# A query projection split in two passes, and an expert gather in groups of two rows

## The reference

```python
q = (hf @ w_q).reshape(T, 8, 2, 128)
s = einsum('thpd,hpnd->thpn', q, sub_keys)          # 128 scores per head and half
sc, idx = top_k(s, 16)                              # per half
cand = sc[..., 0, :, None] + sc[..., 1, None, :]    # 256 pair sums per head
top_sc, pos = top_k(cand, 16)                       # 16 experts per head, 128 per token
gate = softmax(top_sc)
act = gelu(einsum('thkd,td->thk', u_tab[eidx], h))
y = einsum('thk,thkd->td', gate * act, v_tab[eidx])
```

## Time and profile before

| what | value |
|---|---|
| median of 3 runs | 3951.03 us (3946.89 to 3958.45) |
| the profiled execution | 3955.62 us, span 3953.5 us |
| first gather issued / first dot | 2524.75 us / 2539.04 us |
| first dot into slot 8 or above | 2804.9 us (row 72) |
| last dot starts | 3913.04 us (row 511) |
| HBM traffic of the gathers | 536.90 MB |

### The profile page before, as it was taken

The page is one execution under the profiler, slowest core; times in us unless marked ns, Lnnn a source line. Parts: engine busy times, 40 slices in busy tenths (PEclk is TensorE's granted clock), DMA queues, the critical chain, the costliest instruction groups (busy, mean ns, idle before and its releaser), DMA issues. The chain is left out here.

```text
span 3953.5 us, 33526 instructions
## 1 busy us (share of the span) xinstructions
PE 3431.1 (87%) x12069; PEld 2132.3 (54%) x12069; DVE 2296.8 (58%) x4193; ACT 635.4 (16%) x1221; POOL 1878.5 (48%) x1174
## 2 busy tenths in 40 slices
PE   7987999998988999989999889887777777777877
PEld 5435947886655478866877667333333333333333
DVE  3834625445633154447935665456887777777564
ACT  2132222011115221111112331101010000000001
POOL 2212316886510168856877447123444444444442
PEclk9997999999989999999999889988889989999998
DMA  4430012222320123222432211567999999999995
GB/s 142 148 118 1 1 43 73 95 95 78 128 85 1 43 75 95 95 74 75 132 113 84 76 33 54 191 246 295 397 421 421 421 415 419 412 415 417 415 421 236
DMA packets 266249, 741.35 MB, mean 188 GB/s; under 512 B 12921, under 2 KB 192642, under 8 KB 200578
## 3 DMA queue, kind: packets, MB, share of 16 engines
q0 software_dynamic: 73728, 536.90, 33.3%
q1 hardware_dynamic: 188176, 196.15, 15.6%
q10 hardware_dynamic: 4210, 6.56, 0.4%
HBM read 731.17 MB, written 8.39 MB: 187 GB/s over the span
## 5 line engine op out<-in xcount | busy, mean ns | idle before, releaser
L796 POOL TENSOR_TENSOR split_arena<-weight_ring,ones 128x1024 fp32r<-128x1024 f32 x222 | 546.7, 2463 | 686.9 <-PE bank L891 322.6
L854 POOL DMA_INDIRECT arena<-in_peer_uv,rstd x364 | 412.2, 1132 | 643.0 <-PE bank L1354 554.4
L972 PE MATMUL bank<-split_arena 128*128 128x512 f32 x1776 | 698.0, 393 | 0.0
L2369 DVE CUSTOM_DVE_ANT_0 arena<-arena,branch 128x1024 f32<-128x1024 f32 x364 | 443.4, 1225 | 232.3 <-DMA arena<-in_peer_uv,rstd 229.2
L798 POOL TENSOR_TENSOR split_arena<-weight_ring,split_arena 128x1024 fp32r<-128x1024 f32 x222 | 546.2, 2460 | 17.4
L1354 PE MATMUL bank<-arena,level_mask 128*128 128x512 f32 x736 | 370.2, 661 | 109.4 <-DVE level_mask L2354 109.4
L970 PE MATMUL bank<-split_arena 128*128 128x512 f32 x1088 | 427.9, 393 | 17.8 <-DVE split_arena L1803 9.1
L1354 PE MATMUL bank<-arena,row_diagonals 128*128 128x512 f32 x720 | 346.5, 637 | 104.0 <-DVE row_diagonals L2354 104.0
L971 PE MATMUL bank<-split_arena 128*128 128x512 f32 x1088 | 425.1, 391 | 0.0
L972 PEld LDWEIGHTS bank<-split_arena 128*128 128x128 f32 x1776 | 335.5, 189 | 73.8
L891 PE MATMUL bank<-normed,weight_ring 128*128 128x512 f32 (+1 forms) x864 | 362.2, 578 | 5.0 <-DVE normed L1790 3.9
(11 more groups left out here) (346 smaller groups left out, 4937.0 us busy)
## 6 DMA issues: line engine op xcount, KB each, us to landing
weight_ring<-in_w_up SPq DMA_DIRECT2D x32, 1024.0 KB, 5.3
weight_ring<-in_w_down SPq DMA_DIRECT2D x32, 1024.0 KB, 5.1
weight_ring<-in_w_in SPq DMA_DIRECT2D x32, 1024.0 KB, 5.7
weight_ring<-in_ada_w SPq DMA_DIRECT2D x24, 1024.0 KB, 7.7
weight_ring<-in_w_in_a SPq DMA_DIRECT2D x13, 1024.0 KB, 5.3
weight_ring<-in_w_out SPq DMA_DIRECT2D x12, 1024.0 KB, 5.3
weight_ring<-in_w_in_b SPq DMA_DIRECT2D x10, 1024.0 KB, 5.2
weight_ring<-in_peer_wq SPq DMA_DIRECT2D x8, 1024.0 KB, 6.9
```

The costliest lines, as they stand in the source:

```text
L796: pool.tensor_tensor(hi, part, bc_mid(ones[:], DT), ALU.mult).then_inc(split_hi, 1)
L854: pool.indirect_dma_start(row_slots[slot_of[r]], None, a["peer_uv"], bass.IndirectOffsetOnAxis(ap=experts[n % 2][:, c:c + 1], axis=0)).the ...
L972: m = pe.matmul(psum[t.bank][:], hi[:, k, :], a_lo[:, k, :], start=False, stop=k == DT - 1)
L2369: dve.tensor_tensor_reduce(row, row, h_tok[:, r // NE, :], 1.0, 0.0, ALU.mult, ALU.add, dots[:, i % 4, j:j + 1]).then_inc(dot_ready, 1)
```

## The change

- `GROUP` is 2, so there are 256 groups, 64 in a block. `EARLY` is 136.
- The query projection is done twice over. First pass: all 8 units, with the 128 tokens of block 0 as the moving operand; four halves share a bank. Behind each pair of units come the scores of its heads. Second pass: the 8 units are loaded again (8 MB more), and the other 384 tokens are projected in 32 pieces of 4 matmuls, one piece after every second row group (groups 2 to 64).
- The normalised input is made in two parts: 128 columns first, then 384.
- Of the token-major copies of the input (`turn` of `H`) only block 0's is made ahead of the loop; the others come at groups 7 to 27.
- ScalarE evicts a piece, a turn or a score bank three groups after TensorE was to make it (`LAG`).
- Scores of blocks 1 to 3 come one pair of heads at a time, 16 groups apart; their searches run one piece in every second group. The searches of block 0 still to do run one piece per group at groups 0, 10 and 20.
- The sum of a block is taken 2 groups, turned 4 groups and added 8 groups after the block ends.

```diff
-GROUP = 4
+GROUP = 2
-EARLY = 64
+EARLY = 136
+LAG = 3
+PIECES = 8
...
+        query_at = {2 + 2 * y: y for y in range(2 * HP)}
+        turn_at = {7 + 4 * (2 * (n - 1) + i): (n, i) for n in range(1, TT) for i in range(2)}
+        score_at = {(BLK_GRP * (n - 1) + 16 * g + (20 if n == 1 else 28)): (n, g) for n in range(1, TT)
+                    for g in range(PH // SG)}
+        back_at = {BLK_GRP * (n + 1) + 4: n for n in range(TT - 1)}
+        take_at = {BLK_GRP * (n + 1) + 2: n for n in range(TT - 1)}
+        add_at = {BLK_GRP * (n + 1) + 8: n for n in range(TT - 1)}
...
-        for g, at in ((1, 0), (2, 5), (3, 9)):
-            search_at[0, g] = (at, 2)
-        for g in range(PH // SG):
-            search_at[1, g] = (14 + 4 * g, 2)
-            for n in range(2, TT):
-                search_at[n, g] = (BLK_GRP * (n - 1) + 8 * g + 1, 1)
+        search_at = {(0, 1): (0, 1), (0, 2): (10, 1), (0, 3): (20, 1)}
+        for n in range(1, TT):
+            for g in range(PH // SG):
+                search_at[n, g] = (BLK_GRP * (n - 1) + 16 * g + 32, 2)
...
-            for u in pq_units:
+            for u in first_units + rest_units:
                 load(u)
...
                 elif slot_of[r] >= 8:
-                    pool.wait_ge(half_done, 2 * (pq_units[-1].u + 1))
+                    pool.wait_ge(half_done, 2 * (rest_units[-1].u + 1))
...
+            def query_piece(y):
+                x, part = divmod(y, 2)
+                u, h, t = rest_units[x // 2], x % 2, rest_tiles[x]
+                if part == 0:
+                    pe.wait_ge(landed[u.slot], 16 * u.load)
+                    free(pe, t)
+                for k in range(part * DT // 2, (part + 1) * DT // 2):
+                    if x == 0:
+                        normed(k)
+                    m = pe.matmul(psum[t.bank][:, P:], block_of(u, k, h * P), H[:, k, P:], start=k == 0, stop=k == DT - 1)
+                if part:
+                    m.then_inc(half_done, 1)
+
+            for g, t in enumerate(first_tiles):
+                for x in range(2 * SG):
+                    u, h = first_units[SG * g + x // 2], x % 2
...
+                    for k in range(DT):
+                        if g == 0 and x == 0:
+                            normed(k)
+                        m = pe.matmul(blk(psum[t.bank], x), block_of(u, k, h * P), H[:, k, 0:P], start=k == 0, stop=k == DT - 1)
+                    m.then_inc(half_done, 1)
                 if g == 0:
-                    for n in range(TT):
-                        for i in range(2):
-                            turn(tok_turns[n][i], [blk(H[:, 4 * i + j, :], n) for j in range(4)])
+                    for i in range(2):
+                        turn(tok_turns[0][i], [blk(H[:, 4 * i + j, :], 0) for j in range(4)])
                 key_scores(0, g)
...
-            for i in range(2 * SG * 2):
+            for i in range(NGRP):
                 sum_rows(i)
-                query_tile(2 * SG * 2 + i)
+                if i in query_at:
+                    query_piece(query_at[i])
+                if i in turn_at:
...
+                if i in score_at:
+                    key_scores(*score_at[i])
...
             for i in range(NGRP):
                 act.wait_ge(dot_ready, GROUP * (i + 1))
                 act.activation(row_act[:, i % 4, :], dots[:, i % 4, :], ACT.Gelu).then_inc(gelu_ready, 1)
-                if i < 4 * SG:
-                    x = 4 * SG + i
-                    take(pq_tiles[x], pq_f[:, x, :])
+                if i - LAG in query_at and query_at[i - LAG] % 2:
+                    x = query_at[i - LAG] // 2
+                    t = rest_tiles[x]
+                    full(act, t)
+                    act.activation(pq_f[:, x, P:], psum[t.bank][:, P:], ACT.Copy).then_inc(bank_out[t.bank], 1)
...
-            modulate(1)
+            for cols in (slice(0, P), slice(P, SEQ)):
+                marks = []
+                for k in range(DT + 1):
...
-            for t in tok_turns[0] + tok_turns[1] + tok_turns[2] + tok_turns[3]:
-                have(dve, t)
             for _ in search(0, 0):
                 pass
```

More of the change, by code:

```diff
@@ L399, in build @@
             if g == 0:
[L400 to L405, removed]
-        for n in range(TT):
[L407 to L410, removed]
+                tok_turns[0] = [aux(2 + i) for i in range(2)]
@@ new lines, in build @@
+            peer_scores[0].append(aux(4 + g % 2))
+        rest_units = query_units()
+        rest_tiles = [half_tile(u, h, 6 + h) for u in rest_units for h in range(2)]
+        query_at = {2 + 2 * y: y for y in range(2 * HP)}
[3 more added lines that the diff above has]
+        back_at = {BLK_GRP * (n + 1) + 4: n for n in range(TT - 1)}
@@ L411, in build @@
+        peer_back.append([aux(2 * ((TT - 1) % 2) + i) for i in range(2)])
         norms.append(aux(4))
@@ L1333, in key_scores @@
                 free(pe, t)
-                for x in pq_tiles[4 * i:4 * i + 4]:
+                for x in rest_tiles[4 * i:4 * i + 4] if n else first_tiles[i:i + 1]:
                     have(pe, x)
@@ new lines, in _ @@
+            for g, t in enumerate(first_tiles):
+                for x in range(2 * SG):
+                    u, h = first_units[SG * g + x // 2], x % 2
+                    if h == 0:
+                        pe.wait_ge(landed[u.slot], 16 * u.load)
+                    if x == 0:
+                        free(pe, t)
+                    for k in range(DT):
[3 more added lines that the diff above has]
+                    m.then_inc(half_done, 1)
@@ new lines, in _ @@
+                if i in turn_at:
+                    n, x = turn_at[i]
+                    turn(tok_turns[n][x], [blk(H[:, 4 * x + j, :], n) for j in range(4)])
+                if i in score_at:
+                    key_scores(*score_at[i])
+                if i in back_at:
+                    n = back_at[i]
+                    for x in range(2):
+                        have(pe, row_sums[n][x])
+                        turn(peer_back[n][x], [y_sum[:, (4 * x + j) * P:(4 * x + j + 1) * P] for j in range(4)])
@@ L1393, in _ @@
+            for x in range(2):
+                have(pe, row_sums[TT - 1][x])
+                turn(peer_back[TT - 1][x], [y_sum[:, (4 * x + j) * P:(4 * x + j + 1) * P] for j in range(4)])
+            pre[0] += 1
             norm_sum(norms[5])
@@ L2367, in _ @@
                     row = row_slots[slot_of[r]][:, 0:D]
+                    if r % NE == 0:
+                        for t in tok_turns[r // NE]:
+                            have(dve, t)
                     dve.wait_ge(row_landed[slot_of[r]], 16 * fill[r])
```

119 lines of the change are left out of this document (55 added, 64 removed).

## The result

The changed kernel takes 3886.6 us (median of 4 runs, 3882.8 to 3889.9) against 3950.9 us for the kernel before on the same chip: a ratio of 0.9835, 95% interval 0.9816 to 0.9853. That is 1.65% faster, where 2.1% (3869 us) was forecast. The profiled execution took 3889.9 us with a span of 3888.2 us; before the span was 3953.5 us, so 65.3 us have gone where the prediction had 82.9.

A forecast was written before the change was run, and what follows sets the result against it. DMA engines bound it, at 2.524 us per gathered row: 2539.2 + 503 x 2.524 + 15 + 10 = 3833.8 us, + 36.8 = 3870.6 us span, + 2.1 = 3872.7 us profiled, so median 3869 us; range 3828 to 3940 us.

The forecast's parts named there:

- step 4: Rows 8 to 135 in eight slots: DMA-bound at 2.65 us a row, 15 us for second-pass bytes, 10 us for bursts.
- Step 1: Start of the gathers: block 0's input made first brings the search 23 us earlier, the first gather to 2501.6 us.
- Step 2: The first dot waits for unit 7, its load taken as 15.9 us: 2525 us, only 14 us earlier than before.
- Step 3: First slot that comes free: 8.4 us from first dot to re-use of slot 0, row 8 ready at 2539.2 us.
- rival (a): Eight slots stay too few: rows 8 to 135 keep 3.69 us each, 3992 us, slower; chance 0.06.
- blocked gelu: Early rows of the kernel before: ScalarE waits 136.2 us for query halves, so the next gelu, diagonals and sums are late.
- rival (b): Eight-slot rows, half of the lag: smaller groups help nothing, 3.34 us per row, 3947 us, no change; chance 0.05.
- Step 5: The rest, from row 136, where slots 8 to 11 come: 376 rows at 2.524 us each, no gain taken.
- rival (d): More is won: unit 7 lands in 5.4 us, rows at 2.49 us, no bursts: 3833 us; chance 0.06.
- Step 6: The end: after the last dot TensorE sums two rows, not four, 3.7 us less, leaving 36.8 us.
- Rival (c): TensorE's clock drops at short gaps between sums: 3881 us, or over 4100 us in the strong form, chance 0.04.

The follow-up runs named there:

- hold experiment: The changed kernel, with GpSimd issuing no gather until query unit 7, the last of the first pass, has landed: 3879.6 us, ratio 0.9809 to the kernel before.
- late takes: The kernel before, with ScalarE taking each query half, and the score banks behind it, one group later: 3926.6 us, ratio 0.9936.

## Why the prediction was right, and where it was off

The mechanism and the sign were right, and no two errors cancelled: both parts that were off are off the same way. Of the 65.3 us of span, 1.1 lie ahead of the marker and are not the change's; row 8's dot is 5.7 us earlier from the marker; rows 8 to 144 give 54.8, the late rows 0.1, the end 3.5. Expected were 19.5, 59.6, nothing and 3.7. So of the 17.6 us missing, 12.8 are in row 8's dot (2552.0 us, 2539.2 said) and 4.8 in the eight-slot rows. (Two slips of arithmetic in the prediction change nothing: the round trip of step 4 adds up to 14.5 us, not 14.7, and 3872.7 less 4.6 is 3868, not 3869.)

**Step 1, the first gather: right.** 2500.12 us, 2501.6 said.

**Step 2, the first dot: the term that was mis-sized.** 2536.1 us, 2525 said. The chain was right (unit 7's load, its matmuls, 3.3 us to the dot), two of its numbers were not:

- the load took 25.0 us, not 15.9 (9.1 us more; it was issued 0.5 us earlier than worked out);
- unit 7's 32 records took 6.15 us and not 3.8 (2.3 us), since TensorE came out of 19.09 us of idle time (its granted clock from 2520 to 2540 us is 0.67): unit 6's 32 records took 3.84 us, as the timeline above shows.

2501.6 + 25.0 + 6.15 + 3.3 = 2536.1. Why 25.0: beside queued gathers a weight load moves slowly all the way. The queues of the changed kernel from 2510 to 2524 us (gathers, then weight loads; packets, MB, share):

```profile
q0 software_dynamic: 695, 5.06, 87.7%
q1 hardware_dynamic: 696, 0.70, 14.8%
```

The weights got 0.70 MB in 14 us, one byte in eight, 50 GB/s; at that pace a load of 1.05 MB takes 21 us. The load of the earlier trace rows with 15.9 us was issued 11 us into the gathers of the kernel before. The last of the eight landed at 2550.3 us, and the load 1.3 us behind it: its slow part had been cut short. Here it is issued with the first gather, and nearly all eight pass beside it (the last lands at 2527.7 us, the load at 2526.6). I had read a duration from a row without reading how long the stream would stand beside it. It is a share and not a place in line: with the loads cut to an eighth their median time to landing in the eight-slot rows is 7.0 us, not 25.4. The hold experiment has the same: a load of the second pass was issued at 2515.3 us, just behind the start of the gathers, and took 25.8 us, while the loads with no gathers about them took 5.4 to 6.4 us.

The Trainium skill's "DMA: Bandwidth & Descriptors", section "Queues, rings and completion order", has the engines take turns between queues packet by packet. The trace agrees: 695 packets of the one queue and 696 of the other in the 14 us above. From the packets' sizes of the prediction the estimate by this rule would be 17 us of gathers and 2.5 of the load itself, some 20 us; the 25.0 measured decides, and is longer. What the other 4 to 5 us are is open.

**Step 3, the first slot back: right in size.** From first dot to re-use 8.9 us (8.4 said), from re-use to row 8's dot 6.9 (5.8 said). It came late because the dot did.

**Step 4, eight slots: right, the bytes' price a fifth too small.** 373.1 us for 136 rows are 343.3 at the late pace and 29.8 more. 15 were given to the second pass's bytes, at the gathers' 415 GB/s; their own DMA time is 18.5 us (6.29 MB, above), and the experiment with the cut loads bears it out. The rest is 11.3 us, where 10 were given to bursts; I did not split it further. The new evictions do wait for nothing (in the wait table after, ScalarE's wait is for dots), and with the lag set to 0 it costs 28 to 31 us.

**My reason against rival (a) weighed its two parts wrongly.** I wrote that most of the eight-slot stretch's price was the blocked gelu. In the kernel before, rows 0 to 71 take 84 us more than at the late pace (265.9 - 72 x 2.524), and the late takes win 23 to 29 of them: a third, not most. In the changed kernel the lag is worth 28 to 31 us and the group size 73 to 76. With groups of four, the changed kernel is on rival (b)'s and (a)'s ground (3.21 us per row for 136 rows; 3963 us against their 3947 and 3992). So what defeated these rivals is first the group size, and the gelu in second place: the verdict on (a) and (b) was right, the reason given for it in part wrong.

**Step 5 and rival (d): right, no gain.** The late rows are paced by the DMA engines (share 1.01): 2.524 us each, and the 367 rows from row 144 on take 925.4 to 927.1 us in every kernel that ran. The first row with a slot above the eight is 144, as it was 72 before, not 136 as the step has it.

**Step 6, the end: right.** 3888.2 - 3851.3 = 36.9 us (36.8 said). The sums behind the last dot are now those of two rows (the second line below; the first is the pair before), in place of four rows in 7.13 us; they end 6.5 us after the last dot begins, where 6.1 were said and 9.8 it was:

```profile
3850.63 3.70 PE L1371 MATMUL bank<-arena,row_diagonals 128*128 128x512 f32 x8 [1.23 <-DVE row_diagonals L2382]
...
3854.17 3.60 PE L1371 MATMUL bank<-arena,level_mask 128*128 128x512 f32 x8
```

**Rival (c), the clock: small.** A sum of 8 records takes 3.70 us behind a gap of 1.2 us (first line above) and 3.60 with no gap (second line); the clock over the late rows is 0.95. Where the gap is longer, the sum is slower: 5.75 us after 6.30, 5.40 after 4.81 (timeline above). Between 2552 and 2925 us five sums took over 4.2 us (5.2 to 6.8), each behind 3.4 to 4.8 us of idle time; all others took 3.6 to 3.7. So about 2 us were lost five times, and not 1.7 us in every second group, and TensorE had room for it: the DMA share there is 0.99. The Trainium skill's page "TensorE: Matmul & The Clock Gate", section "A second HAM failure mode: psum-queue depth-cycling", has short idles between groups of matmuls make the clock swing. The trace agrees for the gaps of 3.4 us and more; of gaps of 1.2 us it shows no loss.

## What to carry over

When a change lets a large stream start earlier, list every small load that is still to be issued then, and price it by the pace that it gets beside the stream (here 50 GB/s, where a load of 1 MB that takes 5.4 us alone took 25), not by its duration elsewhere. Better, move those loads ahead of the stream, into buffers that the stream has not filled yet (here 23 to 26 us, half of it for the wait and half for bytes that no longer share the stream's time). With few slots, the number of rows that wait for one another decided more here than the engines' load: eight slots in groups of four leave the DMA engines idle for a tenth of the time, in groups of two hardly at all. And judge an early start by the idle time of the engine that bounds the kernel: an earlier dot or slot counts only as far as the windows show that the DMA engines would otherwise have been idle.

## What the hardware showed that I had not expected

- A weight load of 1 MB issued with the first gathers landed in 25.0 us, and in the eight-slot rows in 25.4 in the median (7.3 to 26.4; the one of 7.3 us met only 193 packets of gathers beside its own 1040). It took 15.9 in the kernel before with 11 us of the gathers gone by, and 5.3 to 6.5 one at a time without gathers. While both queues had work they moved 695 and 696 packets in 14 us: the small packets of the weights got 0.70 MB, the gathers 5.06.
- Gaps of TensorE of 1.2 us between sums showed no loss of clock: 3.70 us for 8 records, 3.60 with no gap. After 4.81 us of idle time they took 5.40, after 6.30 they took 5.75.
- With the DMA engines full, bytes of another queue cost the gathers their own DMA time, 16.0 us for 5.5 MB by the queue's share and 16.6 us in the timing. In packets of about 1 KB that is 2.9 us per MB, against 2.5 for the gathered rows.
